# Second mixers: small products in five banks, compression's weights later, both branches' halves in turn, the output product by token tile

## The reference, cut to what matters

```python
h = _rms(x, mix_norm[l])
(q_a, g_a, kc, vc, ks_, vs_, kw, vw, q_b, k_b, v_b, gate_a, gate_b) = _split_cols(h @ w_in[l])
y_a = _nsa(q_a, g_a, kc, vc, ks_, vs_, kw, vw, ...) @ w_branch_nsa[l]
y_b = _moba(q_b, k_b, v_b) @ w_branch_moba[l]
merged = jax.nn.sigmoid(gate_a) * y_a + jax.nn.sigmoid(gate_b) * y_b
x = x + merged @ w_out[l]
```

## Time and profile before

| what | value |
|---|---|
| three runs | 2864.95, 2864.95, 2858.27 us (median 2864.95) |
| the profiled execution | 2863.4 us, span 2861.5 us |
| TensorE busy | 2668.1 us (93%) |
| VectorE busy | 1982.5 us (69%) |
| ScalarE busy | 1550.9 us (54%) |
| mean granted clock of TensorE | 0.957 |

### The profile page before, as it was taken

One profiled execution on the slowest core, in us unless ns is written; L12 is line 12 of the kernel. 1 busy time (PEld: TensorE's weight loads), 2 busy tenths in 40 slices (PEclk: granted clock), 3 DMA queues, 4 the chain that ended last, 5 costly groups with the idle time before them and its releaser, 6 DMA issues.

```text
span 2861.5 us, 38958 instructions
## 1 busy us (share of the span) xinstructions
PE 2668.1 (93%) x15384; PEld 2311.5 (81%) x15384; DVE 1982.5 (69%) x2853; ACT 1550.9 (54%) x2238; POOL 29.1 (1%) x40
## 2 busy tenths in 40 slices
PE   7688998978999999999996998998999999998998
PEld 3677988856888888888885997887898998787898
DVE  4768878886798899889896556555555556555555
ACT  2443444553777778777774444464444444364444
POOL 0000000020000000000000000000000000000000
PEclk9789998989999999999998999999999999999999
DMA  8537974614799999999995664433565664433563
GB/s 279 188 96 283 343 273 123 193 40 130 274 368 341 335 355 355 332 336 368 339 356 167 190 187 154 126 96 111 178 184 167 193 183 145 155 96 110 162 185 118
DMA packets 349599, 616.34 MB, mean 215 GB/s; under 512 B 20705, under 2 KB 174881, under 8 KB 349409
## 3 DMA queue, kind: packets, MB, share of 16 engines
q1 hardware_dynamic: 346402, 603.35, 63.1%
q0 software_dynamic: 1872, 5.99, 0.7%
q10 hardware_dynamic: 1136, 4.44, 0.4%
HBM read 612.66 MB, written 1.05 MB: 214 GB/s over the span
## 4 chain that ended last, share of the span: by engine, by line
PE 80%; DVE 11%; ACT 5%; DMA 2%; issue 2%; SPq 0%; DVEq 0%; ACTq 0%
PE pb L286 23%; PE pb L288 23%; PE pb L287 23%; PE pb L292 8%; DVE parts L260 3%; PE pb L408 2%; ACT parts L245 2%; DVE mod L1657 1%; DMA raw<-in_w_in 1%; PE pb L2609 1%; PE pb L2154 1%; DVE raw L625 1%; DMA raw<-in_ffn_w_up 0%; DMA X<-in_x 0%; DVE hTl L421 0%
## 5 line engine op out<-in xcount | busy, mean ns | idle before, releaser
L260 DVE TENSOR_TENSOR parts<-raw,parts 128x1024 fp32r<-128x1024 f32 (+2 forms) x1051 | 1263.7, 1216 | 614.9 <-ACT parts L245 580.4
L245 ACT ACTIVATE parts<-raw 128x1024 fp32r<-128x1024 f32 (+2 forms) x1051 | 1101.6, 1054 | 832.4 <-PE pb L288 693.9
L286 PE MATMUL pb<-parts,arenar 128*128 128x512 f32 (+2 forms) x1696 | 667.1, 393 | 12.6 <-DVE arenar L421 6.0
L287 PE MATMUL pb<-parts,arenar 128*128 128x512 f32 (+2 forms) x1696 | 649.9, 383 | 0.0
L288 PE MATMUL pb<-parts,arenar 128*128 128x512 f32 (+2 forms) x1696 | 649.5, 383 | 0.0
L286 PE MATMUL pb<-hTh,parts 128*128 128x256 f32 x1952 | 558.2, 286 | 6.0 <-DVE hTl L421 3.5
L287 PE MATMUL pb<-hTl,parts 128*128 128x256 f32 x1952 | 557.0, 285 | 0.0
L288 PE MATMUL pb<-hTh,parts 128*128 128x256 f32 x1952 | 556.8, 285 | 0.0
L286 PEld LDWEIGHTS pb<-hTh,parts 128*128 128x128 f32 x1952 | 379.7, 195 | 9.8 <-issue 5.2
L286 PEld LDWEIGHTS pb<-parts,arenar 128*128 128x128 f32 x1696 | 321.7, 190 | 76.9 <-issue 16.4
L287 PEld LDWEIGHTS pb<-hTl,parts 128*128 128x128 f32 x1952 | 379.7, 195 | 1.8
(11 more groups left out here) (286 smaller groups left out, 1996.5 us busy)
## 6 DMA issues: line engine op xcount, KB each, us to landing
raw<-in_moe_w_gate SPq DMA_DIRECT2D x176, 512.0 KB, 5.2
raw<-in_moe_w_up SPq DMA_DIRECT2D x176, 512.0 KB, 5.2
raw<-in_moe_w_down SPq DMA_DIRECT2D x176, 512.0 KB, 5.2
raw<-in_ffn_wg SPq DMA_DIRECT2D x88, 512.0 KB, 4.1
raw<-in_ffn_wu SPq DMA_DIRECT2D x88, 512.0 KB, 3.8
raw<-in_ffn_wd SPq DMA_DIRECT2D x88, 512.0 KB, 4.4
raw<-in_ada_wT SPq DMA_DIRECT2D x80, 512.0 KB, 5.2
raw<-in_w_in SPq DMA_DIRECT2D x72, 512.0 KB, 3.7
```

The lines of the kernel that those rows point to most:

```text
L245: a.e.activation(self.part(t, 0), self.slot(t), ACT.Copy).then_inc(*a.up(self.c.hi, t.m))
L260: v.e.tensor_tensor(self.part(t, 1), self.slot(t), self.part(t, 0).bitcast(F32), ALU.subtract).then_inc(*v.up(self.c.lo, t.m))
L286: e.matmul(o, a[0], b[0], start=start, stop=False, skip_group_check=True)
L287: e.matmul(o, a[0], b[1], start=False, stop=False, skip_group_check=True)
```

## The change

Four things, in both layers alike.

1. The front's small products go to banks 3, 4, 5, 6 and 7 instead of 7 alone. Both block transposes stand at (1, 1). The compression's first product goes from (2, 0) to (2, 1), in bank 5; the second stays at (2, 3), in bank 3. Their small products go to (3, 0) and (3, 1). The transposes of ks go to (2, 2), those of kw to (5, 0). VectorE's parts move with them: the rope of kw's tile 1 to (4, 0), its copy to (4, 1), and `w2_dve` to (3, 2) and (3, 3).
2. The compression's weights stand four loads later in SyncE's order.
3. The branches' eight loads alternate (`branches_pe`): ya half 0 twice, yb half 0 once, ya half 1 once, yb half 0 again, ya half 1 again, then yb half 1 twice. O's second half is transposed in two pairs of k rows, both token tiles at once. m's first half is transposed after the seventh load, in banks 7 and 6, its second half after the second load of wo, in banks 7 and 1.
4. The output product (`out_pe`) does both column halves over the first half of m, then all four remaining loads for token tile 0, then for token tile 1. Both adds to X follow there.

```diff
@@ tiles @@
-        t[2] = t[2][:2] + self.cmp_tiles(0) + t[2][2:]
-        t[3] = t[3][:2] + self.cmp_last(0) + t[3][2:3] + self.cmp_tiles(1) + t[3][3:]
-        t[4] = t[4][:1] + self.cmp_last(1) + t[4][1:]
+        t[3] = t[3][:2] + self.cmp_tiles(0) + t[3][2:] + self.cmp_tiles(1)
+        t[4] = t[4][:1] + self.cmp_last(0) + t[4][1:2] + self.cmp_last(1) + t[4][2:]
...
+        t.append([ya[0], ya[1], yb[0], ya[2], yb[1], ya[3], yb[2], yb[3]])
+        return sum(t, []) + [wo[i] for i in (0, 1, 4, 5, 2, 3, 6, 7)]
@@ fill_pe @@
         if at == (1, 1):
             self.blocks_pe(t, 7, 0)
-        elif at == (1, 2):
-            self.blocks_pe(t, 7, 1)
-        elif at == (2, 0):
-            self.w1_pe(t, 7, 7, 0)
+            self.blocks_pe(t, 6, 1)
+        elif at == (2, 1):
+            self.w1_pe(t, 5, 7, 0)
         elif at == (2, 2):
-            self.w2_pe(t, 7, 7, 0)
+            self.group_pe(t, 4, "ks")
         elif at == (2, 3):
-            self.w1_pe(t, 7, 7, 1)
+            self.w1_pe(t, 3, 6, 1)
         elif at == (3, 0):
-            self.group_pe(t, 7, "ks")
+            self.w2_pe(t, 7, 5, 0)
         elif at == (3, 1):
-            self.w2_pe(t, 7, 7, 1)
+            self.w2_pe(t, 6, 3, 1)
         elif at == (3, 2):
-            self.heads_pe(t, 7, "qa", 0)
+            self.heads_pe(t, 5, "qa", 0)
...
+        elif at == (10, 0):
+            self.pair_pe(t, 0)
+        elif at == (10, 2):
+            self.pair_pe(t, 1)
+        elif at == (10, 6):
+            self.m_pe(t, 0)
@@ fill_dve @@
         elif at == (3, 1):
-            self.w2_dve(v, 7, 1)
             self.rope_dve(v, "qa", 8, 1)
         elif at == (3, 2):
-            self.copy_dve(v, "kw", "ks")
+            self.w2_dve(v, 7, 0)
+        elif at == (3, 3):
+            self.w2_dve(v, 6, 1)
         elif at == (4, 0):
             self.keys_dve(v, 7)
+            self.rope_dve(v, "kw", 2, 1)
         elif at == (4, 1):
             self.scores_dve(v, 7, 0)
+            self.copy_dve(v, "kw", "ks")
...
+        elif at == (10, 0):
+            self.pair_dve(v, 0)
+        elif at == (10, 2):
             for tt in range(2):
-                self.turned_dve(v, "O", tt, 4)
+                self.ya_dve(v, 0, tt)
+            self.pair_dve(v, 1)
+        elif at == (10, 4):
+            for tt in range(2):
+                self.yb_dve(v, 0, tt)
+        elif at == (10, 5):
+            for tt in range(2):
+                self.ya_dve(v, 1, tt)
+        elif at == (10, 6):
+            self.m_dve(v, 0)
+        elif at == (10, 7):
+            for tt in range(2):
+                self.yb_dve(v, 1, tt)
@@ banks @@
-        b = {("O", 0): 7, ("O", 4): (5, 7)[tt], ("m", 0): 6, ("m", 4): 7}[name, k0]
+        b = {("O", 0): (7, 7), ("m", 0): (7, 6), ("m", 4): (7, 1)}[name, k0][tt]
...
     def ya_banks(self, i):
-        return self.banks(10 + i)
+        return (2, 0) if i == 0 else (1, 2)
 
     def yb_banks(self, i):
-        return (3, 4) if i == 0 else (0, 1)
+        return (3, 4) if i == 0 else (0, 5)
@@ the branches and the output product on TensorE @@
+    def branches_pe(self, t):
+
+        K = self.K
+        for s, (name, i, k0) in enumerate((("ya", 0, 0), ("ya", 0, 2), ("yb", 0, 0), ("ya", 1, 0), ("yb", 0, 2),
+                                           ("ya", 1, 2), ("yb", 1, 0), ("yb", 1, 2))):
+            x = self.load(t, name, i, k0)
+            if name == "ya":
+                self.turned_ready(t, "O", 0)
+                self.tile_pe(t, name, i, x, self.OT_lhs, self.ya_banks(i))
+            else:
+                self.pair_ready(t, k0 // 2)
+                self.tile_pe(t, name, i, x, lambda k, tt: K.hT_lhs(4 + k, tt), self.yb_banks(i))
+            self.fill_pe(t, 10, s)
+
+    def out_pe(self, t):
+
+        K = self.K
+        for i, k0 in ((0, 0), (0, 2), (1, 0), (1, 2)):
+            x = self.load(t, "wo", i, k0)
+            self.turned_ready(t, "m", 0)
+            self.tile_pe(t, "wo", i, x, K.hT_lhs, self.wo_banks(i), last=6)
+            if (i, k0) == (0, 2):
+                self.m_pe(t, 512)
+        loads = [(i, self.load(t, "wo", i, k0)) for i in range(2) for k0 in (4, 6)]
+        self.turned_ready(t, "m", 4)
+        for tt in range(2):
+            for i, x in loads:
+                self.tile_pe(t, "wo", i, x, K.hT_lhs, self.wo_banks(i), (tt,), 6)
```

More of the change, by code:

```diff
@@ L2998, in yb_dve, with add_dve @@
         v.e.tensor_tensor(x, x, u, ALU.add).then_inc(*v.up(K.c.dv, self.key("m", c, tt)))
-    def add_dve(self, v, tt, i=1):
-        K, c = self.K, 512 * i
-        b, x = K.c.bk[self.wo_banks(i)[tt]], K.X[:, tt, c:c + 512]
-        v.wait_ge(*K.c.pe.val((self.key("wo"), c, tt)))
-        v.e.tensor_tensor(x, x, b.t[:, :], ALU.add).then_inc(*v.up(b.out, (self.key("wo"), c, tt)))
+    def add_dve(self, v, tt):
+        K = self.K
+        for i in range(2):
+            c = 512 * i
+            b, x = K.c.bk[self.wo_banks(i)[tt]], K.X[:, tt, c:c + 512]
+            v.wait_ge(*K.c.pe.val((self.key("wo"), c, tt)))
+            v.e.tensor_tensor(x, x, b.t[:, :], ALU.add).then_inc(*v.up(b.out, (self.key("wo"), c, tt)))
     def x_ready(self, q, tt, h):
@@ L3012, in OT_lhs, with tile_pe, load @@
         return tuple(h[:, k, tt * P:(tt + 1) * P] for h in self.OT)
+    def tile_pe(self, t, name, i, load, lhs, banks, tts=(0, 1), last=2):
+        K, c, name = self.K, 512 * i, self.key(name)
+        k0, m, (h, l) = load
+        for tt in tts:
+            b = K.c.bk[banks[tt]]
+            if k0 == 0:
+                t.wait_ge(*b.turn((name, c, tt)))
+            for j in range(2):
+                x = mm3(t.e, b.t[:, :], lhs(k0 + j, tt), (h[:, j, :], l[:, j, :]), k0 + j == 0, k0 + j == last + 1)
+            keys = [("w", m)] if tt else []
+            if k0 == last:
+                keys.append((name, c, tt))
+            if keys:
+                x.then_inc(*t.up(K.c.pe, *keys))
+    def load(self, t, name, i, k0):
+        return (k0, *self.K.W.take(t, (self.key(name), 512 * i, k0)))
+    def branches_pe(self, t):
[11 more added lines that the diff above has]
+    def out_pe(self, t):
+        K = self.K
+        for i, k0 in ((0, 0), (0, 2), (1, 0), (1, 2)):
[9 more added lines that the diff above has]
+                self.tile_pe(t, "wo", i, x, K.hT_lhs, self.wo_banks(i), (tt,), 6)
     def pe(self, t):
@@ L3074, in act @@
                 self.fill_act(a, i, s)
-        for i in (10, 11):
-            for s in range(2):
-                K.W.hi(a)
-                self.fill_act(a, i, s)
-        K.W.hi(a, 2 + 1)
-        self.m_act(a, 0)
-        K.W.hi(a, 1 + 1)
+        for s in range(8):
+            K.W.hi(a)
+            self.fill_act(a, 10, s)
+        K.W.hi(a, 2)
         self.m_act(a, 512)
-        K.W.hi(a, 3)
+        K.W.hi(a, 2)
     def dve(self, v, add, norm):
```

119 lines of the change are left out of this document (53 added, 66 removed).

## The result

The changed kernel takes 2816.19 us (median of four runs, 2814.02 to 2818.59), beside 2863.4 us for the kernel before (four runs, 2858.27 to 2864.95). The ratio is 0.9838, with a 95% interval of 0.9821 to 0.9855: faster by 47 us. The waits went as forecast; the clock gave back more than I had allowed for.

A forecast was written before the change was run, and what follows sets the result against it. TensorE, busy for 2668.1 of 2861.5 us, bounds the kernel, losing time to waits for VectorE and half clock. 2863.4 - 20.6 (waits) - 13.5 (clock) = 2829.3, forecast 2829 us; range for 8 in 10: 2819 to 2847.

The forecast's parts named there:

- Step 1: Front, both blocks at once in banks 7 and 6: the waits for L2597, 2.8 and 2.7 us, go.
- Step 2: Front, compression's weights four loads later, its products in two banks: waits of 1.5 and 2.5 us go.
- Step 3: Front, q's rope: 0.35 us per layer goes, about 1.7 us of waiting stays; work moved into the attention costs 0.
- Step 4: Ends, alternating branch halves: 8.0 us of waits go, two new ones of 1.4 us come, 5.2 us gained per layer.
- Step 5: End, output product by token tile: no change in time, 0 us.
- The clock term: Fronts and ends: of 22.7 us lost to half clock, 7.7 and 1.5 us stay lost, 13.5 us won.
- (a): Fronts and ends: the clock stays as it was, only the waits' 20.6 us come, 2843 us; chance 0.17.
- (b): Branches: VectorE becomes the bound, new waits 3.5 us each instead of 1.4, 2844 us; chance 0.13.
- (c): Whole change: nothing won, new waits replace removed ones and late weights stop TensorE, 2860 to 2866 us; chance 0.05.
- (d): Branches and output product: new waits and transposes keep the clock at half, slower, 2917 us; chance 0.03.

The follow-up runs named there:

- e6: Changed kernel with the second block transposes back in bank 7, a load after the first, putting one wait back per layer: 2835.84 us.
- e5: Changed kernel with the compression's weights back at their old place in SyncE's queue, new banks and fill order kept: 2840.7 us, ratio 0.9939.
- e1: Kernel before with only the new front (five banks, later compression weights), branches and output product old: 2839.75 us, ratio 0.9926.
- e10: Changed kernel with ya's first half multiplied earlier, its second half after m's low parts, and the output product's banks moved: 2814.49 us, ratio 0.984.
- e4: Changed kernel without any edit, profiled once more: 2824.27 us.
- e7: Changed kernel with the compression's 16 thin products run twice over, no wait added: 2851.26 us.
- e2: Changed kernel with the old fronts, so only branches, output product and m's banks are new: 2841.26 us, ratio 0.9922.
- e3: Kernel before without any edit, profiled once more: 2861.88 us.
- e12: Changed kernel with both token tiles of each half of m in one bank again, as before: 2836.26 us.
- e8: Kernel before with 2 instead of 16 thin products per compression product, the waits kept: 2854.05 us.
- e9: Changed kernel with the rope of q one load sooner on VectorE: 2814.42 us, ratio 0.985.

## Where the prediction was right, and the step that failed

**Step 1 (blocks in two banks): right.** The wait is gone in both layers, and the first product of the compression waits for nothing. e6 adds what the step left out: such a wait can cost, beside its 2.5 us, 5 us of clock.

**Step 2 (late weights): right in its sum, too modest in its meaning.** The waits of 1.5 and 2.5 us went, SyncE's pause with them, and no load came late: where the earlier trace rows show ScalarE idle for a DMA, its waits over the second front (2376 to 2429 us) name no DMA:

```profile
ACT parts L245 <- PE pb L288: 22.4, 13, 5.3
```

Its copies wait for TensorE alone. e5 shows that the front's gain needs this step: without it the new banks and the new order have waits of 4.5 and 2.4 us of their own.

**Step 3 (rope): right.** 1.74 and 1.75 us are left, 1.7 forecast. VectorE's timeline shows the chain with the copy gone, beside the earlier trace rows: rope of tile 0, low part, rope of tile 1, back to back.

```profile
2416.77 0.76 DVE L2541 TENSOR_TENSOR arena<-arena,cst 128x256 f32<-128x256 f32 x2
...
2418.91 1.22 DVE L260 TENSOR_TENSOR parts<-raw,parts 128x1024 fp32r<-128x1024 f32 x1
2420.23 0.76 DVE L2541 TENSOR_TENSOR arena<-arena,cst 128x256 f32<-128x256 f32 x2
```

The work moved into the attention cost no length at a given clock: with 3.4 us at half clock it takes 128.4 us with the moved work (e1's and e10's first, both of e4) and 128.4 without (before). The half-clock time itself was higher with it: 0 to 10.2 us, 4.5 on average, in the 18 stretches behind a front with late weights and new banks, and 0 or 3.4, 2.1 on average, in the eight behind an old front. That is (4.5 - 2.1) / 2 = 1.2 us of time per layer (an estimate), which the step had at nothing. Whether the moved work causes it was not tried.

**Step 4 (the ends): right.** Two new waits came where they were forecast, of 1.24 and 1.34 us (1.4 and 1.4 forecast), so 5.5 us went per layer (8.04 - 2.58) and not 5.2.

**Step 5 (output product by tile): right.** The stages behind the ends take 399.4 and 203.6 us, 399.7 and 203.5 before.

The idle time comes to 20.9 us; 20.6 were forecast. Each part of that sum is within 0.3 us.

**The clock term failed.** The step was: "I let half of the fronts' 30.9 us stay (7.7 us lost), and one short stretch per end region", 13.5 us won. Measured in the mixers: 20.0 us. In this execution none of it stayed in the fronts and none in the ends, and the attention took 6.8 us of half clock more, 3.2 us of time. The reason I gave for keeping half, that "the product runs remain", was sound in kind: e7 shows the thin products bringing the clock down with no wait. Its size was wrong. In the 14 fronts that keep the runs and lose the long waits 13.6 us of half clock are left in all, 1.0 us per front, where I had left 15.5 for the two. I had taken the second run of the earlier trace rows for what a run does; it stood behind a wait. The rows of before did not settle this. The run with no wait just ahead stood at 1.00 in the second layer, but in the first layer the same run stood at 0.88, 4.6 us behind the wait for L2597:

```profile
1770.90:1775.00 4.10, 4.10 (x34) 4.07 (x33) 1.86 (x5) 2.34 (x2) 0.00 (x0) 0.88 0.00 0
```

For the ends, one short stretch each was kept with no reason given; 18 of 18 ends without waits over 1.4 us have none.

The prediction also set the clock gate's moment as run-variable, after the Trainium skill (TensorE: Matmul & The Clock Gate, Part 1: The HAM clock gate), so that this term could be anything "whatever the waits do". The page says it of the slow products at a kernel's start; in the middle of this one the ends contradict it: 18 of 18 ends without waits over 1.4 us had no half clock at all, and all 8 with the old waits had 6.8 to 13.7 us. How much half clock follows a wait does vary (13.7 to 17.1 us in the six old fronts of before, e2 and e3). The same page, in its section "A second HAM failure mode: psum-queue depth-cycling", says that frequent small idle gaps between groups of products, as banks of PSUM are cycled, make the clock swing. The old ends agree: four waits for banks of 1.3 and 2.7 us, 10.2 and 6.8 us at half clock, and none without them. Read so, the whole term would have gone with the waits: 22.7 us, nearer to the measured 20.0 than my 13.5.

What the step missed is 6.5 us. Of the 12.8 us between forecast and profile, it and three others make up 12.7: the 5.6 us ahead of the first mixer, which are chance and no part of the change (e3, e4), 0.3 between the mixers, and 0.3 in the waits. So nearly half of the distance was chance, and the clock term most of the rest. My range ended 2.8 us above the measured time, because its lower end is about the sum with the whole clock term won (2863.4 - 20.6 - 22.7 = 2820.1) and left nothing for chance elsewhere.

Of the rivals, (a) (the clock stays, 2843) is refuted by the fronts' 1.00 and the ends'; (b) (VectorE becomes the bound, 2844) by waits of 1.3 instead of 3.5 us; (c) by the result, though e5 shows what it would look like in the front; (d) by both ends at 1.00.

## What to carry to other kernels

Where a product engine waits for 2 us and more, count the clock with the wait: here a removed microsecond of idleness gave back nearly another of half clock. Where one engine issues all loads in order, look for a load whose slot is freed late, and move that one behind loads that are wanted sooner: without that, new banks and a new order gained nothing in the front (e5). And a new order with old buffers can gain almost nothing (e12), so change both and then undo each.

## What was unexpected of the hardware

Waits of 1.2 to 1.8 us left the clock alone: in 14 ends with two such waits and in 14 fronts with one, it did not fall in the 14 us behind any of them. Of the 28 waits of 2.0 to 4.5 us in the fronts of before, e2, e3, e5, e6 and e8, 23 had the clock fall during the wait or within 1.3 us of its end.

TensorE counts as busy all through a run of thin products, and yet the clock can fall in it: in four of four runs of 64 instructions, and in three of 28 runs of 32 with no long wait in the front. e9's 6.8 us began in such a run.

Why those three runs and not the other 25 is open, and so is the attention, with 0 to 10.2 us of half clock in each stretch although its waits are the same. A front or an attention moves by 2 to 5 us with this from one execution to the next, so a small gain is read from stages and not from whole times.
